# Layer norms relative to a four-tile mean, and the first two panels behind a norm taken together

## What is computed

```python
def layer_norm(x, g, b):
    mu = jnp.mean(xf, axis=-1, keepdims=True)
    var = jnp.mean(jnp.square(xf - mu), axis=-1, keepdims=True)
    return (xf - mu) * lax.rsqrt(var + LN_EPS) * g + b

for layer in range(2):                      # first block
    u = x * (1.0 + scale) + shift
    y = even_mixer(u, ...) if layer == 0 else fox_attention(u, ...)
    x = layer_norm(ALPHA * x + gate * y, ln_g[layer, 0], ln_b[layer, 0])
    u = x * (1.0 + scale) + shift
    y = square(relu(u @ mlp_w1[layer] + mlp_b1[layer])) @ mlp_w2[layer] + mlp_b2[layer]
    x = layer_norm(ALPHA * x + gate * y, ln_g[layer, 1], ln_b[layer, 1])
# second block: two hybrid layers, each followed by a gated feed-forward
# (gate, up, down); rms_norm ahead of both, and one at the end
```

## Time and profile before

| | |
|---|---|
| median of 3 runs | 2976.16 us (2976.15 to 2983.06) |
| the profiled execution | 2995.0 us |
| its span, first to last instruction | 2993.5 us |
| granted TensorE clock over the span | 0.964 of full speed |
| VectorE busy | 1626.0 us |
| ScalarE busy | 1107.9 us |
| GpSimd | no arithmetic on tiles; 17 DMA issues |

### The profile page before, as it was taken

The page is one execution under the profiler, slowest core; times in us unless marked ns, Lnnn a source line. Parts: engine busy times, 40 slices in busy tenths (PEclk is TensorE's granted clock), DMA queues, the critical chain, the costliest instruction groups (busy, mean ns, idle before and its releaser), DMA issues.

```text
span 2993.5 us, 38213 instructions
## 1 busy us (share of the span) xinstructions
PE 2807.2 (94%) x15546; PEld 2228.9 (74%) x15546; DVE 1626.0 (54%) x2878; ACT 1107.9 (37%) x1904; POOL 9.4 (0%) x21
## 2 busy tenths in 40 slices
PE   5788999989998899997998999999989989999998
PEld 4666888866666688884886777888868767678887
DVE  6678646553555665655445665444545475443334
ACT  3444324234554432424334443222334443432222
POOL 0000000000000000000000000000000000000000
PEclk9999999999998999998999999999999997999999
DMA  6345555532221365662230013444422200122322
GB/s 239 123 134 168 187 179 181 183 113 74 68 71 50 115 202 183 197 197 70 92 113 9 2 50 120 141 144 137 159 98 92 71 2 2 64 92 94 98 98 85
DMA packets 92077, 336.10 MB, mean 112 GB/s; under 512 B 10480, under 2 KB 10736, under 8 KB 91776
## 3 DMA queue, kind: packets, MB, share of 16 engines
q1 hardware_dynamic: 86800, 315.40, 32.3%
q10 hardware_dynamic: 3792, 14.05, 1.3%
q0 software_dynamic: 1312, 4.23, 0.5%
HBM read 331.50 MB, written 2.13 MB: 111 GB/s over the span
## 4 chain that ended last, share of the span: by engine, by line
PE 87%; DVE 7%; ACT 4%; DMA 1%; issue 1%; ACTq 0%; DVEq 0%
PE bank L626 23%; PE bank L628 22%; PE bank L627 22%; PE bank L800 2%; PE bank L825 2%; PE bank L811 2%; DVE in_low L1243 1%; DVE hidden L1246 1%; PE bank L899 1%; PE bank L643 1%; PE bank L674 1%; PE bank L644 1%; PE bank L645 1%; PE bank L1109 1%; DMA weight_ring<-stream 1%
## 5 line engine op out<-in xcount | busy, mean ns | idle before, releaser
L626 PE MATMUL bank<-in_high,weights_high 128*128 128x512 f32 x2144 | 865.0, 403 | 48.4 <-DVE in_low L1243 39.0
L627 PE MATMUL bank<-in_low,weights_high 128*128 128x512 f32 x2144 | 846.2, 395 | 0.0
L628 PE MATMUL bank<-in_high,weights_low 128*128 128x512 f32 x2144 | 845.9, 395 | 0.0
L1153 DVE TENSOR_TENSOR weights_low<-weight_ring,weights_high 128x1024 fp32r<-128x1024 f32 x404 | 494.0, 1224 | 459.9 <-ACT weights_high L1790 459.9
L1790 ACT ACTIVATE weights_high<-weight_ring 128x1024 fp32r<-128x1024 f32 x404 | 424.4, 1051 | 474.2 <-PE bank L628 320.5
L626 PEld LDWEIGHTS bank<-in_high,weights_high 128*128 128x128 f32 x2144 | 409.5, 191 | 183.4 <-issue 58.7
L628 PEld LDWEIGHTS bank<-in_high,weights_low 128*128 128x128 f32 x2144 | 409.3, 191 | 87.6
L627 PEld LDWEIGHTS bank<-in_low,weights_high 128*128 128x128 f32 x2144 | 410.5, 191 | 84.8 <-issue 3.6
L626 PE MATMUL bank<-hidden_split,weights_high 128*128 128x512 f32 x864 | 336.1, 389 | 0.0
L627 PE MATMUL bank<-hidden_split,weights_high 128*128 128x512 f32 x864 | 336.1, 389 | 0.0
L628 PE MATMUL bank<-hidden_split,weights_low 128*128 128x512 f32 x864 | 336.1, 389 | 0.0
(11 more groups left out here) (340 smaller groups left out, 2859.0 us busy)
## 6 DMA issues: line engine op xcount, KB each, us to landing
weight_ring<-stream SPq DMA_DIRECT2D x597, 512.0 KB, 3.5
mixer_out<-cmp ACTq DMA_DIRECT2D x6, 1024.0 KB, 4.9
hidden<-forget_rows POOLq DMA_DIRECT2D x16, 256.0 KB, 3.8
residual<-x ACTq DMA_DIRECT2D x4, 512.0 KB, 12.9
mixer_out<-cmp SPq DMA_DIRECT2D x2, 1024.0 KB, 6.6
out<-mixer_out ACTq DMA_DIRECT2D x4, 512.0 KB, 2.7
constants<-consts ACTq DMA_DIRECT2D x1, 1757.5 KB, 20.8
silu_c<-c ACTq DMA_DIRECT2D x2, 512.0 KB, 4.4
```

The costliest lines, as they stand in the source:

```text
L626: pe.matmul(bank[:, :], WHI[:, z, cols], high, start=(k == 0), stop=False)
L627: pe.matmul(bank[:, :], WHI[:, z, cols], low, start=False, stop=False)
L628: ins = pe.matmul(bank[:, :], WLO[:, z, cols], high, start=False, stop=(k == ktiles - 1))
L1153: v.tensor_tensor(WLO[:, z, :], ring[:, n % RING, :], WHI[:, z, :].bitcast(F32), ALU.subtract).then_inc(*mark("weights_low", "low", n))
```

## The change

Each layer norm is computed relative to a shift s, the mean of the first four tiles of X, which is known while the last three panels run. After panel 4 TensorE multiplies the sum of X[0..3] with a constant 2/D (`mean4`) into bank 2 (`ln_shift`). VectorE subtracts s from X[5..7] before their last addition (`ln_pre`, 3 instructions) and from X[0..4] (`ln_shifted`, 5). ScalarE squares the shifted tiles during the last panels and GpSimd sums squares 0 to 6, six additions a norm (`ln_squares`). Behind the last panel the mean takes two matmuls and the mean square two; the variance is the mean square less the squared mean (`ln_rest`, `ln_v`). The 8 subtractions of the mean stay. The root of norms 0 and 2 moves from `TMP` to M[7], and the 8 scalings of X move from the end of those norms into the first 8 panels of the MLP.

Behind norm 3 ScalarE squares the scaled X with the bias added in the same instruction, TensorE averages the 8 squares directly, and GpSimd adds the bias to X (8 additions).

Behind six norms (0, 2, and the first four RMS norms of the second block) the first two panels run together (`gemm_pair`): tile k of the first, then tile k-2 of the second, in two banks.

```diff
+    LN_SUM, LN_SQUARES, LN_LAST, LN_REST, LN_VAR = M[:, 0, :], M[:, 1, :], M[:, 2, :], M[:, 3, :], M[:, 4, :]
+    ln_square_tile = lambda k: LN_LAST if k == KT - 1 else M[:, 1 + k, :]
+    ln_root = lambda i: M[:, 7, :] if i in (0, 2) else R
...
+        def gemm_pair(keys, x, ready):
+            banks, used = [gemm_bank(key) for key in keys], [PANELS[key][0] for key in keys]
+            for n in used:
+                pe.wait_ge(*at("low", n))
+            for k in range(KT + 2):
+                for bank, n, j in zip(banks, used, (k, k - 2)):
+                    if not 0 <= j < KT:
+                        continue
+                    if j == k:
+                        pe.wait_ge(*at(*ready(k)))
+                    z, cols = split_turn[n] % NSPLIT, slice(j * P, j * P + P)
+                    high, low = x(j)
+                    pe.matmul(bank[:, :], WHI[:, z, cols], high, start=(j == 0), stop=False)
+                    pe.matmul(bank[:, :], WHI[:, z, cols], low, start=False, stop=False)
+                    ins = pe.matmul(bank[:, :], WLO[:, z, cols], high, start=False, stop=(j == KT - 1))
+                    if j == KT - 1:
+                        ins.then_inc(*mark("panels_used", "used", n))
+                        ev.also("panels_used", "gemm", keys[used.index(n)])
...
+        def ln_shift(i):
+            pe.wait_ge(*at("ln_sum4", i))
+            ins = pe.matmul(B[2][:, :], const("mean4"), LN_SUM, start=True, stop=True)
+            ins.then_inc(*mark("tensor_means", "ln_s", i))
...
+            pe.wait_ge(*at("ln_part", i))
+            pe.matmul(B[2][:, :], const("mean"), LN_SUM, start=True, stop=False, skip_group_check=True)
+            pe.wait_ge(*at("res", i, KT - 1))
+            ins = pe.matmul(B[2][:, :], const("mean"), X[:, KT - 1, :], start=False, stop=True, skip_group_check=True)
+            ins.then_inc(*mark("tensor_means", "ln_mean", i))
+            pe.wait_ge(*at("ln_sumsq", i))
+            pe.matmul(B[3][:, :], const("mean"), LN_SQUARES, start=True, stop=False, skip_group_check=True)
+            pe.wait_ge(*at("ln_square", i, KT - 1))
+            ins = pe.matmul(B[3][:, :], const("mean"), LN_LAST, start=False, stop=True, skip_group_check=True)
+            ins.then_inc(*mark("tensor_means", "ln_var", i))
...
+                if m == 4:
+                    ln_shift(i)
...
+                if half == 0:
+                    gemm_pair([("up", l, 0, 0), ("up", l, 0, 1)], u_split, lambda k: ("norm_out", "ln", i - 1, k))
+                for j in range(2 if half == 0 else 0, HALF):
+                    gemm(("up", l, half, j), u_split)
...
+            gemm_pair(ropes[0:2], u_split, lambda k: ("norm_out", "mix", l, k))
+            turn(0)
+            for i in range(2, 5):
...
+                    if j == 0:
+                        gemm_pair([("gate", l, 0), ("gup", l, 0)], u_split, lambda k: ("norm_out", "ffn", l, k))
...
-        mean_square(("in", 0))
+        for k in range(KT):
+            pe.wait_ge(*at("x_square", "in", 0, k))
+            mean_step(B[3], H[:, 24 + k, :], k, ("ms", "in", 0))
...
+        def ln_sum4(i, m):
+            if 1 <= m <= 3:
+                v.wait_ge(*at("res", i, m))
+                v.tensor_tensor(LN_SUM, X[:, 0, :] if m == 1 else LN_SUM, X[:, m, :], ALU.add).then_inc(
+                    *(mark("residual", "ln_sum4", i) if m == 3 else step("residual")))
...
+        def ln_shift(i, m, alpha):
+            if m == 4:
+                v.wait_ge(*at("ln_s", i))
+                for k in range(5, KT):
+                    if alpha is None:
+                        v.wait_ge(*at("half_res", i, k))
+                        v.tensor_tensor(X[:, k, :], X[:, k, :], B[2][:, :], ALU.subtract).then_inc(
+                            *mark("vector_norm", "ln_pre", i, k))
+                    else:
+                        v.scalar_tensor_tensor(X[:, k, :], X[:, k, :], alpha, B[2][:, :], ALU.mult, ALU.subtract).then_inc(
+                            *mark("vector_norm", "ln_pre", i, k))
+                for k in range(5):
+                    v.wait_ge(*at("res", i, k))
+                    v.tensor_tensor(X[:, k, :], X[:, k, :], B[2][:, :], ALU.subtract).then_inc(
+                        *mark("vector_norm", "ln_shifted", i, k))
...
+                v.wait_ge(*at("res", i, m))
+                v.wait_ge(*(at("ln_shifted", i, 4) if m == 5 else last("ln_parts")))
+                v.tensor_tensor(LN_SUM, X[:, 4, :] if m == 5 else LN_SUM, X[:, m, :], ALU.add).then_inc(
+                    *(mark("ln_parts", "ln_part", i) if m == 6 else step("ln_parts")))
...
+            v.wait_ge(*at("ln_rest", i))
             for k in range(KT):
-                v.wait_ge(*at("res", i, k))
+                if k == 3:
+                    v.wait_ge(*at("ln_var", i))
+                    v.tensor_tensor(LN_VAR, B[3][:, :], LN_REST, ALU.subtract).then_inc(*mark("vector_norm", "ln_v", i))
+                v.wait_ge(*(at("ln_shifted", i, k) if k < 5 else at("res", i, k)))
                 v.tensor_tensor(X[:, k, :], X[:, k, :], B[2][:, :], ALU.subtract).then_inc(
...
+            if i in (1, 3):
+                for k in range(KT):
+                    ln_scale(i, k, gcol_)
...
+                if ready is not None:
+                    v.wait_ge(*at(*ready, k))
+                v.scalar_tensor_tensor(H[:, STAGE + k, :], X[:, k, :], gain(k), root, ALU.mult, ALU.mult).then_inc(
...
+                    if half == 0 and j < KT:
+                        ln_scale(i - 1, j, vec1("ln_g", 8 * i - 8, 8 * i))
...
-                        v.wait_ge(*at("half_res", i, m))
+                        v.wait_ge(*(at("half_res", i, m) if m < 5 else at("ln_pre", i, m)))
                         gated(("down", l, 1, m), m, mod[:, 16:24], ("res", i, m))
-                        partial_sum("residual", M[:, 0, :], lambda k: X[:, k, :], m, ("ln_mean", i))
+                        ln_sum4(i, m)
+                        ln_shift(i, m, None)
...
+                    v.wait_ge(*at("evicted", key(m)))
+                    v.wait_ge(*at("ln_pre", i, m))
+                    v.tensor_tensor(X[:, m, :], X[:, m, :], TMP[:, m % 2, 0:T], ALU.add).then_inc(
+                        *mark("residual", "res", i, m))
+                ln_sum4(i, m)
+                ln_shift(i, m, ALPHA)
...
+                if m == KT - 1:
+                    ln_square(i, 6)
                 residual(key(m), m, mod[:, 16:24], bias, ("res", i, m - 2) if m > 1 else None)
+                if m == 5:
+                    for k in range(5):
+                        ln_square(i, k)
+                if m == 6:
+                    ln_square(i, 5)
+        def ln_square(i, k):
+            s.wait_ge(*(at("ln_shifted", i, k) if k < 5 else at("res", i, k)))
+            if k == KT - 1:
+                s.wait_ge(*at("ln_added", i, 1))
+            s.activation(ln_square_tile(k), X[:, k, :], ACT.Square).then_inc(*mark("scalar_norm", "ln_square", i, k))
...
-            for k in range(KT):
-                s.wait_ge(*at("ln_centre", i, k))
-                s.activation(M[:, k, :], X[:, k, :], ACT.Square).then_inc(*mark(sem, "ln_square", i, k))
-            s.wait_ge(*at("ln_var", i, KT - 1))
-            inv_sqrt(sem, B[3], 1e-5, R, ("ln_r", i))
+            ln_square(i, KT - 1)
+            s.wait_ge(*at("ln_mean", i))
+            s.wait_ge(*at("ln_added", i, 2))
+            s.activation(LN_REST, B[2][:, :], ACT.Square).then_inc(*mark(sem, "ln_rest", i))
+            s.wait_ge(*at("ln_v", i))
+            inv_sqrt(sem, LN_VAR, 1e-5, ln_root(i), ("ln_r", i))
...
-                s.activation(X[:, k, :], X[:, k, :], ACT.Identity, bias=bcol[:, k:k + 1]).then_inc(*mark(sem, "ln_x", i, k))
+                s.activation(H[:, 24 + k, :], X[:, k, :], ACT.Square, bias=bcol[:, k:k + 1]).then_inc(
+                    *mark(sem, "x_square", "in", 0, k))
...
-                    elif j == 0 and half == 0:
-                        s.wait_ge(*at("ln_norm", i - 1, KT - 1))
...
+                        for k in {5: range(5), 6: (5,), 7: (6,)}.get(m, ()):
+                            ln_square(i, k)
...
+        def ln_squares(i):
+            g.wait_ge(*at("ln_square", i, 0))
+            for k in range(1, KT - 1):
+                g.wait_ge(*at("ln_square", i, k))
+                if k > 1:
+                    g.wait_ge(*at("ln_added", i, k - 1))
+                g.tensor_tensor(LN_SQUARES, LN_SQUARES, ln_square_tile(k), ALU.add).then_inc(
+                    *mark("gpsimd_sums", "ln_added", i, k))
+            ev.also("gpsimd_sums", "ln_sumsq", i)
+        ln_squares(0)
+        ln_squares(1)
...
+        ln_squares(2)
+        ln_squares(3)
...
+            g.wait_ge(*at("x_square", "in", 0, k))
+            g.tensor_tensor(X[:, k, :], X[:, k, :], vec1("ln_b", 24 + k, 25 + k).broadcast_to([P, T]), ALU.add).then_inc(
+                *mark("gpsimd_sums", "ln_x", 3, k))
```

53 lines of the change are left out of this document (23 added, 30 removed).

## The result

Both kernels were run five times on one chip. The kernel before: 2981.07 us median (2976.15 to 2983.21). The changed kernel: 2959.18 us median (2954.00 to 2979.47). The ratio is 0.9946, 95% interval 0.9927 to 0.9964. On a second occasion (x_after, the same kernel, seven runs against 22) it was 0.9958, 0.9938 to 0.9978; 0.992 to 0.993 had been expected of that repeat if the scatter fell on both kernels alike, and this did not come. So the change makes the kernel faster, by 0.4 to 0.55% where 0.87% was forecast. The two medians of the first occasion alone lie 21.9 us apart, 0.73%, which is at the edge of that interval; I go by the ratios. The median 2959.18 lies inside the range 2940 to 2962, 9.0 us above the 2950.2 that was forecast.

What follows compares the result with a forecast made beforehand. TensorE, busy 94% of the span, bounds the kernel, so time goes where it waits or runs slowly. Norms 0 to 3 (-0.35, -2.9, -5.8, -8.9) and four pairs (-8.0) sum to -25.95: 2976.16 - 26.0 = 2950.2 us, range 2940 to 2962.

Steps and rivals of the forecast that it cites:

- GpSimd's additions: Six a norm, eight behind norm 3: taken at 1.25 us each, costing nothing up to 1.8 us each.
- 2976.16 - 26.0: Whole kernel: median of the runs before, less the summed saving, gives 2950.2 us.
- The crowding: Before norm 0: eight new VectorE instructions, 5.06 us, do not fit into 2.15; T moves by about +4.6.
- The tail: Layer norms 0 to 2: G comes at T + 10.6, -3.15 in norms 0 and 2, -3.75 in norm 1.
- the pair: First two panels behind norms 0 and 2: third panel at G + 13.0 instead of 16.48, -3.5 each.
- The 1.7 us for the mean at the lower level: Norm 0: TensorE stands still before the mean, takes its three matmuls at the lower level, G 1.7 later.
- The rival: The lock of rival 2: 4 us lost before norm 0; behind norm 3 scalings 1.9 us apart, G at T + 26.
- Norm 2: Sum of +0.87 for the shift's matmul, -3.15 for the tail and -3.5 for the pair: -5.8 us.
- Norm 3: Direct averaging of squares brings G to T + 22.6 against 32.40, -9.8; with +0.87 for the shift's matmul, -8.9.
- Four pairs of the second block: Third panels at G + 13.0 instead of 14.98, -2.0 at each of four places, -8.0 in all.
- rival 5: GpSimd's additions much slower than taken, sum of squares late; outweighs 26 us from 3.4 us each; at 5, 3008; 4%.
- rival 2: GpSimd additions and VectorE instructions with two SBUF inputs exclude each other: 9 us lost over the norms, 2959; 30%.

Runs made afterwards that it cites:

- x_best: Changed kernel with norm 0 as before, second block's vectors loaded earlier and norm 3's bias added on VectorE instead of GpSimd: ratio 0.9916 to the kernel before.
- x_pairs: Kernel before with the six panel pairs alone, norms untouched: median 2976.6 us, ratio 0.9989.
- x_best_fill: x_best with unused float32 matmuls in TensorE's pauses: ratio 0.9863 to the kernel before, 0.9878 when repeated.
- x_vec_early: Changed kernel with the second block's vectors loaded earlier, ahead of norm 3's MLP and at layer 0's feed-forward start: ratio 0.9957 to the kernel before.
- x_scan_warm: Changed kernel with a wide unused matmul before each scores' matmul in the second block's slots 20 to 31: ratio 1.0065 to the kernel before.

## Why the prediction missed

Two steps failed. One is a term put at nothing: GpSimd's additions. They cost 4.8 us at norm 0 and up to 1.6 behind norm 3, by runs without them, and 2.1 at norm 2, by the rows. The other is "2976.16 - 26.0", which took all unchanged code to be the same time in both kernels; in the profiled executions its two longest stretches took 8.0 us more after the change, at a lower granted clock. Term by term, against the profiled executions:

**Norm 0: forecast -0.35, measured about +2.4.** The crowding was nearly right: 4.0 where 4.6 stood. The tail alone is worth 3.4 (13.76 to 10.34) where 3.15 stood, the pair 2.8 where 3.5 stood. The 1.7 us for the mean at the lower level do not come with the crowding; with GpSimd's additions 0.9 come. The step that failed is "GpSimd ... nothing up to 1.8 us each": it asked whether the additions are done in time and not what they take from VectorE, on the one engine that had no room. The rival put 4 us on it, and 3.8 were measured at T. The mechanism is seen in the row, 2.31 us for a modulation of 1.28, and gone without GpSimd. The rule in the Trainium skill, "SBUF — State Buffer", SBUF: two separate sides, is that a VectorE instruction with two SBUF inputs and a GpSimd instruction that reads SBUF exclude each other; the stretched rows agree. An instruction that reads one operand from a bank is not stretched, which agrees too; ahead of norm 1:

```profile
595.26 5.77 POOL L2456 TENSOR_TENSOR mixer_out<-mixer_out 128x512 f32<-128x512 f32 x3 [340.17 <-ACT mixer_out L1965]
595.81 2.31 DVE L1201 TENSOR_TENSOR weights_low<-weight_ring,weights_high 128x1024 fp32r<-128x1024 f32 x1
598.40 0.75 DVE L1262 SCALAR_TENSOR_TENSOR residual<-bank,modulations,residual 128x512 f32<-128x512 f32 x1 [0.29 <-PE bank L635]
```

**Norm 1: forecast -2.9, measured -3.2.** The tail of T + 10.6 was T + 10.34.

**Norm 2: forecast -5.8, measured -6.2.** The number is right by luck. The forecast had no modulations between the panels of this projection, and it has one, before the last panel's addition:

```profile
987.80 1.28 DVE L1162 CUSTOM_DVE_ANT_0 weight_ring<-weight_ring,silu_c,vectors 128x1024 f32<-128x1024 f32 x1
989.01 1.22 DVE L1153 TENSOR_TENSOR weights_low<-weight_ring,weights_high 128x1024 fp32r<-128x1024 f32 x1
```

In the changed kernel GpSimd adds beside these two and they take 2.31 and 2.27 us. TensorE stands still for 2.87 us before the last tile's mean, and from the mean's first matmul to T it is 3.8 us (992.71 - 988.88) instead of 1.7 (993.32 - 991.62): 2.1 lost, and the matmuls of the variance run partly at the lower level (1.64 and 1.92 us, T + 11.04). This is argued from the rows; no run took norm 2's additions out. It does not show in the sum because the place ahead of it, between norms 1 and 2, took 2.0 us less in this profile, with one matmul of 0.87 more, at a granted clock of 0.94 instead of 0.93.

**Norm 3: forecast -8.9, measured -7.5.** T + 24.06 instead of 22.6. Without GpSimd's additions it is T + 22.44, near the sum, which had the share at the lower level right. What ends last in the changed kernel is a wait that I did not have, 2.86 us for a DMA whose issue the stretched scalings delay; to load the vectors earlier is worth 1.3, to leave out the additions 1.6, both together (x_best) 1.6. The rival had T + 26, from scalings 1.9 us apart; they were 1.45 us apart. The last two additions, behind the scalings, took 1.03 us each, so strict turns, each instruction whole, would give 0.67 + 1.03 = 1.7. That is more than the 1.45 measured. So the two overlapped in part, and the rival's lock for the whole instruction does not fit this addition, whose second input is one column.

**Four pairs of the second block: forecast -8.0, measured -8.1.** Third panels at G + 13.0, 13.0, 13.9 and 12.8. Before, they are at G + 15.0 ahead of the feed-forwards and at G + 15.4 ahead of the attentions, where two more matmuls stand in front; the forecast had 14.98 for all four. Behind norms 0 and 2 the forecast gave the pair 3.5 each and named the scalings as what must be gone; x_pairs shows that it is nothing otherwise.

**GpSimd's own time: taken 1.25, measured 1.27 us alone** (1266 ns, the shortest of 24) and up to 2.29 beside VectorE. Ln never waited for the sum of squares, so rival 5 is out.

So the segments gave 23.5 of 26.0; 0.9 of it lies in the output projection and feed-forward of layer 0, for which nothing was forecast. By the ratios the larger miss is the step that is not in the sum at all: **"2976.16 - 26.0"**, which took all other code to be the same time in both kernels. In two stretches of 400 us the clock falls or does not (0.66 over 60 us is 41 us at the lower level, 20 us lost), and the executions of one kernel differ by 20 us through it. By the lowest runs the change gives 22.2 us on the first occasion and 16.4 on the second, by the ratios 16 and 12.5. That the median, 2959.18, is what rival 2 had, 2959, is luck: the additions cost about what it said (8.5 of 9 us), but other terms came out better, so that the segments give 23.5 us where it had 17, and the clock in unchanged code and the low base made up the rest.

**What stays open** is whether the change has a part in that scatter. The kernel before lay 7 us above its lowest run on average (28, 22 and 11 runs) and 5 in another 17; the pairs alone 6.6 (12); the kernels with the new norms 8 to 14 (5, 7, 9, 11, 12 and 6 runs), except norms 0 and 3 undone, 4.6 (6 runs). Fillers brought the changed kernel to 2 (6 runs), left the kernel before at 13 (12 runs) and x_best_fill at 2 and 9 (4 and 6). The more runs a set has, the lower its lowest is likely to be, so small sets look steadier than they are. Pauses alone do not explain these figures. No experiment moved the stretch against its surroundings without changing anything else, and none showed what makes the clock fall there.

## What to carry over

Before moving elementwise work to GpSimd, look at what VectorE does at that moment: where VectorE had idle time the exclusion cost nothing that could be measured (norm 1); where it had none, it cost 4.8 us and made the new scheme a loss at norm 0. Take what stands on VectorE at each place from the trace, a single modulation too, as before norm 2, where the stretched instructions lost 2.1 us. Apply a scheme norm by norm, not to all of them. And before forecasting a change of under 1% from one profile, look at how far runs of the same kernel lie apart and in which stretch; fix that base first, or read the change in segments.

## What was not expected of the hardware

- Beside a GpSimd addition of 128x512, a VectorE instruction with two SBUF tensors took 2.3 us for 1.22 to 1.28 (128x1024) and 1.5 to 1.8 for 0.69 (128x512). Even copies and products on a few columns, 0.16 to 0.19 us otherwise, took 0.94 and 1.02 in x_vec_early.
- TensorE's clock fell while it was 100% busy: 0.50 over 40 us in x_scan_warm. It also falls in pauses, and there filling helped: the average behind norm 3 went from 9.48 to 7.13 us in x_best_fill.
- The fall is at the same place of the same code in different kernels, and there or not there from one execution to the next: over the same 60 us of layer 0, 0.66 in one profile of the changed kernel and 0.97 in the other; in the kernel before, 1.00 in layer 0 and 0.66 in layer 1.
